# Two-layer attention and expert block on one core: row picks for two experts at once, a third place for gate and up weights, a shorter extra block

## The reference

```
def expert_dispatch(h, experts, weights, w_gate, w_up, w_down):
    ...
    def run_block(args):
        xb, e = args
        return (jax.nn.silu(xb @ w_gate[e]) * (xb @ w_up[e])) @ w_down[e]

    ys = lax.map(run_block, (xs, block_expert)).reshape(n_slots, D)
    w_sorted = weights.reshape(n_assign)[order].astype(h.dtype)
    return jnp.zeros((T, D), h.dtype).at[order // TOP_K].add(ys[dest] * w_sorted[:, None])
```

## Time and profile before

| | |
|---|---|
| median of 3 runs | 2093.99 us (2093.91 to 2096.98) |
| the profiled execution | 2094.21 us, its span 2092.4 us |
| TensorE busy | 1866.6 us (89%) |
| VectorE busy | 685.4 us (33%) |
| ScalarE busy | 515.9 us (25%) |
| chain that ended last | TensorE 72%, DMA 11%, VectorE 7% |
| moved by DMA | 550 MB, 263 GB/s over the span |

### The profile page before, as it was taken

The page is one execution under the profiler, slowest core; times in us unless marked ns, Lnnn a source line. Parts: engine busy times, 40 slices in busy tenths (PEclk is TensorE's granted clock), DMA queues, the critical chain, the costliest instruction groups (busy, mean ns, idle before and its releaser), DMA issues.

```text
span 2092.4 us, 27923 instructions
## 1 busy us (share of the span) xinstructions
PE 1866.6 (89%) x9715; PEld 999.2 (48%) x9716; DVE 685.4 (33%) x1467; ACT 515.9 (25%) x1052; POOL 153.1 (7%) x190
## 2 busy tenths in 40 slices
PE   5899999999979999977999589989978989888985
PEld 2666666668743333322333377768933333223323
DVE  2455355445442111111111475573441111111112
ACT  3344444432231101100011254442220101110111
POOL 0035021000000000000000206230000000000000
PEclk8899999999989999998999799999989999999997
DMA  6536565222256999975999333233477989999992
GB/s 219 194 141 218 203 215 206 101 75 91 81 241 281 421 421 421 421 290 237 406 421 420 138 107 96 92 106 111 146 291 311 421 363 421 420 421 421 421 421 98
DMA packets 96042, 550.47 MB, mean 263 GB/s; under 512 B 14162, under 2 KB 15650, under 8 KB 42724
## 3 DMA queue, kind: packets, MB, share of 16 engines
q1 hardware_dynamic: 83108, 526.89, 63.6%
q0 software_dynamic: 4224, 11.35, 1.9%
q10 hardware_dynamic: 8640, 11.28, 1.5%
HBM read 537.15 MB, written 12.32 MB: 263 GB/s over the span
## 4 chain that ended last, share of the span: by engine, by line
PE 72%; DMA 11%; DVE 7%; ACT 4%; issue 3%; SPq 1%; ACTq 0%; DVEq 0%; POOL 0%; POOLq 0%
PE ps L757 18%; DMA moe<-in_w_exp_gate_up_dram 9%; PE ps L479 8%; PE ps L742 8%; PE ps L769 7%; PE ps L481 7%; PE ps L480 7%; PE ps L691 2%; PE ps L647 2%; PE ps L535 2%; PE ps L749 1%; PE ps L618 1%; DVE w_lo L1225 1%; PE ps L629 1%; PE ps L763 1%
## 5 line engine op out<-in xcount | busy, mean ns | idle before, releaser
L757 PE MATMUL ps<-moe,ht 128*64 128x512 f32 x2048 | 451.4, 593 | 22.2 <-DMA moe<-in_w_exp_gate_up_dram 22.2
L757 PEld LDWEIGHTS ps<-moe,ht 128*64 128x64 f32 x2048 | 150.2, 137 | 316.1 <-issue 291.7
L479 PE MATMUL ps<-ht_hi,w_hi 128*128 128x512 f32 (+1 forms) x704 | 252.6, 359 | 1.7 <-ACT arena L1027 1.6
L1526 DVE TENSOR_TENSOR arena<-aux,ps 128x256 f32<-128x256 f32 x64 | 26.9, 421 | 687.3 <-ACT aux L1120 687.3
L481 PE MATMUL ps<-ht_hi,w_lo 128*128 128x512 f32 (+1 forms) x704 | 243.6, 346 | 0.0
L480 PE MATMUL ps<-ht_lo,w_hi 128*128 128x512 f32 (+1 forms) x704 | 243.6, 346 | 0.0
L769 PE MATMUL ps<-moe,arena 128*64 128x512 f32 x1024 | 231.4, 594 | 2.6 <-DVE arena L1547 2.6
L1225 DVE TENSOR_TENSOR w_lo<-ws,w_hi 128x1024 fp32r<-128x1024 f32 (+1 forms) x122 | 149.1, 1226 | 230.7 <-ACT w_hi L933 230.7
L742 PE MATMUL ps<-arena,ht 128*64 128x512 f32 x816 | 211.8, 629 | 4.4 <-DVE ht L1479 4.4
L933 ACT ACTIVATE w_hi<-ws 128x1024 fp32r<-128x1024 f32 (+1 forms) x122 | 125.3, 1027 | 190.2 <-PE ps L481 151.3
L479 PEld LDWEIGHTS ps<-ht_hi,w_hi 128*128 128x128 f32 x704 | 133.1, 189 | 43.7 <-issue 23.9
(11 more groups left out here) (232 smaller groups left out, 2047.8 us busy)
## 6 DMA issues: line engine op xcount, KB each, us to landing
moe<-in_w_exp_gate_up_dram SPq DMA_DIRECT2D x256, 1024.0 KB, 13.4
moe<-in_w_exp_down_dram SPq DMA_DIRECT2D x128, 1024.0 KB, 16.3
moe<-in_w_mod_dram SPq DMA_DIRECT2D x32, 1536.0 KB, 6.9
ws<-in_w_in_dram SPq DMA_DIRECT2D x92, 512.0 KB, 4.1
y_rows<-arena ACTq DMA_DIRECT2D x164, 64.0 KB, 5.6
ws<-in_w_branch_dram SPq DMA_DIRECT2D x16, 512.0 KB, 3.6
ws<-in_w_out_dram SPq DMA_DIRECT2D x16, 512.0 KB, 3.4
aux<-in_rpb_a_dram POOLq DMA_DIRECT2D x64, 64.0 KB, 3.2
```

What stands on the lines that cost most here:

```text
L479: pe.matmul(ps[:, bank, 0:cols], w[:, k, :], a_hi, start=(i == 0), stop=False)
L757: mm = pe.matmul(ps[BLK * j:BLK * j + BLK, bank, :].rearrange("p (g n) -> p g n", g=2), x[:, at:at + BLK], w[:, k, 512 * j:512 * j + 512]. ...
```

## The change

1. `pick` holds two experts (128 columns), is f32r (the one-pass format), and is multiplied with `hr_hi` and `hr_lo`, the token rows split into a rounded part and its remainder. ScalarE makes `hr_hi` in the place of `hr`; VectorE makes `hr_lo` with 2 nt new subtractions, ahead of the rest of its routing chain. `turn_x` and the copies handle the pair: picks in the pair's first expert, turns in its second.
2. `xg`, `xs`, `hid`, `hid_t` and the result buffer are single, and gate/up and down use one PSUM bank each. The freed part of `ht` and the weight buffer `ws` of the mixer form a third place for gate and up, used by expert 2 alone. The first four experts of each layer are unrolled for that (the first six in the list of loads).
3. The first extra block stands outside its loop, and the loop runs only if a second is needed. It picks with f32r too, 32 columns by 512.
4. `yg` has four places, and no fetch waits for another.

```
-AHEAD = 3
+AHEAD = 4
+PAIRS = NE // 2
+AHEAD_PAIRS = 2
...
+        wgu = [[part(moe, 32 * i + 8 * j, 8, 2, D) for j in range(4)] for i in range(2)]
+        wgu.append([part(ws_flat, 8 * j, 8, 2, D) for j in range(3)] + [part(ht_flat, 0, 8, 2, D)])
+        wd = [[part(moe, 64 + 16 * i + 8 * j, 8, 2, D) for j in range(2)] for i in range(2)]
...
+                load_gate_up(lambda w: w[l, 2], 2, range(3))
+                sp.wait_ge(g["hturn_done"].sem, g["hturn_done"].at(l, 2 * (width(l) // P) - 1))
+                load_gate_up(lambda w: w[l, 2], 2, (3,))
...
+                next_gate_up(3, 1, 0)
+                next_down(2, 0)
+                next_gate_up(4, 0, 1)
+                next_down(3, 1)
+                next_down(4, 0)
+                next_gate_up(5, 1, 3)
+                next_down(5, 1)
+                with sp.Fori(3, PAIRS) as two:
+                    for s in range(2):
+                        next_gate_up(2 * two + s, s, 2 * two + s - 2)
+                        next_down(2 * two + s, s)
...
+                def pick_x(half):
+
+                    for tile in range(nt):
+                        for rows in (hr_hi, hr_lo):
+                            mm = pe.matmul(ps[:, 7 * half, :], pick[:, tile, :], rows[:, tile, 512 * half:512 * half + 512],
+                                           start=(tile == 0 and rows is hr_hi), stop=(tile == nt - 1 and rows is hr_lo))
...
+                        more_block(BLK // MORE)
+                        with pe.If(n > BLK + MORE):
+                            with pe.Fori(BLK // MORE + 1, w_all // MORE) as b:
+                                with pe.If(n > b * MORE):
+                                    more_block(b)
+                                pe.nop(nofuse=True)
+                        pe.nop(nofuse=True)
+                    pe.nop()
+                    if s == 0:
+                        pe.wait_ge(g["pick_set"].sem, pick0 + two + 2)
+                    else:
+                        pe.wait_ge(g["xs_copied"].sem, pair0 + two + 2)
+                    next_pair = turn_x if s else pick_x
+                    next_pair(0)
+                    pe.wait_ge(g["hid_done"].sem, done + 1)
+                    turn_h(hid)
+                    next_pair(1)
+                    pe.wait_ge(g["hidt_copied"].sem, done + 1)
+                    pe.wait_ge(g["y_copied"].sem, done + 1)
+                    down(4, hid_t, wd[s], g["down_done"].sem)
...
+                for n in range(2 * nt):
+                    dve.wait_ge(g["hr_hi_set"].sem, g["hr_hi_set"].at(l, n))
+                    cols = slice(512 * (n % 2), 512 * (n % 2) + 512)
+                    v.tensor_tensor(hr_lo[:, n // 2, cols], ps[:, n % 6, :], hr_hi[:, n // 2, cols].bitcast(F32), ALU.subtract) \
+                        .then_inc(g["hr_lo_set"].sem, g["hr_lo_set"].tick(l, n))
...
                 for tile in range(nt):
-                    if tile >= 2:
-                        pool.wait_ge(g["comb"].sem, g["comb"].at(l, tile - 2))
```

More of the change, by code:

```diff
@@ L269, in hybrid_block, with gu_slot, gu_loads @@
         bias_in = [g[f"bias{i}"] for i in range(4)]
[L270 to L274, removed]
+        gu_in, wd_in = [g[f"gu_in{i}"] for i in range(3)], [g[f"wd_in{i}"] for i in range(2)]
+        yg_got = [g[f"yg_got{i}"] for i in range(4)]
+        def gu_slot(e):
+            return e if e < 3 else 1 - e % 2
+        def gu_loads(slot, before=NE):
+            return sum(gu_slot(e) == slot for e in range(before))
         def width(l):
@@ L713, in _ @@
                 mm.then_inc(g["logits_done"].sem, g["logits_done"].tick(l))
[L714 to L721, removed]
+                for n in range(2 * nt):
+                    bank = n % 6
+                    claim(bank)
+                    for c in range(4):
+                        mm = pe.transpose(ps[:, bank, c * P:(c + 1) * P], ht[:, 4 * (n % 2) + c, n // 2 * P:(n // 2 + 1) * P], ident[:, :])
+                    mm.then_inc(g["hturn_done"].sem, g["hturn_done"].tick(l, n))
+                    free[bank] = (g["hr_lo_set"], (l, n))
                 msk = r[:, 1024:1024 + 64].bitcast(BF16).rearrange("p (t e) -> p t e", e=NE)
@@ L734, in _ @@
                 pe.wait_ge(g["routed"].sem, g["routed"].at(l))
[L736 to L741, removed]
-                            mm = pe.matmul(ps[BLK * j:BLK * j + BLK, 0, :], picks[:, tile, :], hr[:, tile, 512 * j:512 * j + 512],
-                                           start=(tile == 0), stop=(tile == nt - 1))
-                    if tile == nt - 1:
+                pe.wait_ge(g["hr_lo_set"].sem, g["hr_lo_set"].at(l, 2 * nt - 1))
@@ L843, in _ @@
+                for e in range(2 * AHEAD_PAIRS):
+                    expert(e, e // 2, e % 2, gu_slot(e), gu_loads(gu_slot(e), e + 1))
+                with pe.Fori(AHEAD_PAIRS, PAIRS) as two:
+                    for s in range(2):
+                        expert(2 * two + s, two, s, 1 - s, two + s)
                 after = (l + 1, "n1") if l + 1 < DEPTH else (l, "fin")
-                pe.wait_ge(y_copied[1].sem, 16 * (l + 1) + 1)
+                pe.wait_ge(g["y_copied"].sem, NE * (l + 1) + 1)
@@ L1147, in _ @@
-                        with act.If(n > HALF):
-                            save_rows(ysb[s], act.snap(row + HALF, min_val=0, max_val=2 * NTOK), g["yt_saved"], first=HALF, rows=HALF)
-                            act.reg_add(n_tails, n_tails, 1)
-                        act.nop()
-                act.wait_ge(y_saved[0].sem, 32 * 16 * (l + 1) + 32)
-                act.wait_ge(y_saved[1].sem, 32 * 16 * (l + 1) + 32)
+                    act.nop()
+                    act.wait_ge(g["down_done"].sem, done + 1)
@@ new lines, in expert @@
+                    nc.scalar.activation(ysb, ps[:, 4, :], ACT.Copy).then_inc(g["y_copied"].sem, 1)
+                    act.wait_ge(g["y_copied"].sem, done + 2)
+                    act.wait_ge(g["yo_saved"].sem, act.snap(n_more, min_val=0, max_val=64) * 64 + 64)
+                    save_rows(ysb, row, g["y_saved"], rows=HALF)
+                    with act.If(n > HALF):
+                        save_rows(ysb, act.snap(row + HALF, min_val=0, max_val=2 * NTOK), g["yt_saved"], first=HALF, rows=HALF)
+                        act.reg_add(n_tails, n_tails, 1)
@@ L1153, in _ @@
+                    act.nop()
+                with act.Fori(0, PAIRS) as two:
+                    for s in range(2):
+                        expert(2 * two + s)
+                act.wait_ge(g["y_saved"].sem, 32 * NE * (l + 1) + 32)
                 act.wait_ge(g["yt_saved"].sem, act.snap(n_tails, min_val=0, max_val=64) * 32 + 32)
@@ L1552, in add_tile @@
+                with dve.Fori(0, PAIRS) as two:
+                    for s in range(2):
+                        expert(2 * two + s, two, s)
                 def add_tile(tile):
```

333 lines of the change are left out of this document (160 added, 173 removed).

## The result

| | before | changed |
|---|---|---|
| median | 2094.36 us (2093.91 to 2096.98, 4 runs) | 2081.49 us (2080.59 to 2084.38, 4 runs) |
| ratio | | 0.9933 (95% interval 0.9919 to 0.9948) |
| the profiled execution, its span | 2094.21, 2092.4 us | 2084.38, 2082.6 us |
| layer 0, first expert load to the end of expert 31's `down` | 569.0 us | 556.5 us |
| layer 1, the same | 528.8 us | 531.0 us |

The change makes the kernel 12.9 us faster where 33 was forecast. Layer 0 gained 12.5 us of 26.4, layer 1 lost 2.2 where 6.0 of gain was counted. The profiled execution is 2.9 us above its median.

What follows compares the result with a forecast made beforehand. TensorE set layer 0's pace and the weight loads, at 421 GB/s, late layer 1's, so idle load-queue time counted. Gains of 26.4 (layer 0), 6.0 (layer 1) and 0.8 (fetches) made 33 off 2094.2: 2061 us, range 2046 to 2085.

Steps and rivals of the forecast that it cites:

- the skip over the extra block: TensorE's jump past both copies of the extra block in experts not needing it; the sum gave it no cost.
- rival A: Jumping over the extra block's two copies costs a code fetch: 30 us slower than before, 2124 us; chance 10%.
- The price: Code fetch for each layer's first six experts: 5.6 us, like a small store under full loads; decisive from 3.1 per expert.
- The clock: TensorE's clock in new waits of up to 4.4 us per pair: should it fall, the sum stays; no separate chance.
- f32r picks 0.227 us apart: Spacing of the 16 pick products serving two experts: 3.63 us per pair in layer 0, 1.82 in layer 1.
- TensorE's pace: TensorE's time per expert pair: 27.1 us in layer 0, 26.2 in layer 1, against the loads' 31.3 and 30.5.
- Extra block: Layer 0's block after gate and up: 16.7 us instead of 21.2, 18.0 in a pair's first expert; layer 1 14.9 and 16.2.
- Start: Subtractions before each layer's first pick delay expert 0's gate and up by 6.5 us in layer 0, 4.8 in layer 1.
- Third place: Extra gate/up buffer moves 4 MB, 10 us of transfer, into idle time at each layer's start; without it, 26 us gain.
- Gathers: Tile fetches: the third tile's wait of 0.83 us goes, 0.8 us less.
- shorter extra blocks and the pick make most of it: Claim on where the gain comes from: without the third gate/up buffer the same count still gives 26 us less.

Runs made afterwards that it cites:

- the dead copies: The kernel before plus a never-run second copy of the extra block in TensorE's code of both loop experts, kept in the program: 2115.65 us, ratio 1.0093.
- the rolled kernel: The changed kernel with all 16 pairs per layer in the loop and two places for gate and up, extra block still twice: 2066.52 us, ratio 0.9854.
- the fourth of the experiments: The changed kernel with two places for gate and up instead of three, first four experts still unrolled: 2083.74 us, ratio 0.9946.

## Why the prediction was wrong, point by point

*The step that failed is the skip over the extra block.* The sum put it at nothing, and the fetch that it needs stood only in rival A, at 10%. It measured 24.3 us of gaps in ten places, and 20 us of the time come back with one copy in place of two. I had cited against it the 46 packets and the first passes without a gap. Both were true, and of another jump: one over a single copy. By the timeline's counts a copy of the extra block is 121 products in the changed kernel's layer 0 and as many weight loads (16 + 8 + 64 + 1 + 32), so 242 instructions, and in before 262. The changed kernel jumps over two copies, some 480. One copy was free in before and nearly free in the experiments (at most two gaps of 1.4 to 2.5 us in a kernel); two cost a gap at the first time behind every expert that skipped both, but for the first of a layer.

The Trainium skill (Runtime: NRT & Kernel Launch, Instruction fetch mechanics) gives blocks of 256 instructions, a window of two, and a forced fetch for a jump that leaves it. The traces agree in two points: the dead copies, 984 instructions in all (two of 262 and two of 230), bring 4 packets more, and most jumps over some 480 instructions had a gap of up to 3.0 us, those over 262 none and those over 242 few. They differ on the window: the four copies in the rolled kernel's loop are 968 instructions, and it ran all later passes with no gap and 50 packets for the whole program, so more than two blocks stayed. The section also says that kernels prefer full unrolling where possible. No run here shows a gain from unrolling alone, and with two copies it cost 17.2 us (2083.74 against 2066.52).

*The price* was set at 5.6 us by the nearest row, with the turn at 3.1 per expert. It was 1.6 to 2.9 us behind gate and up, for five experts of layer 0 and four of layer 1 in place of six each. The same count with 2 us in each of six experts gives a gain of 13.0, and with 3 us one of 1.3, both estimates; the gain was 12.9. So the mechanism of A came true and its sign did not: I had taken a fetch as either absent or as dear as a landing store, with no case at half that price.

*The clock* "is no rival of its own" held where I had looked: in the load-bound part of layer 1 gate and up take 8.49 us after a wait of 2.64, and the pair still 30.55. It failed behind the gaps, where the low-clock `down` (4.50) and picks (0.43 apart) stand among the experts that TensorE sets the pace of. By how much it adds to the loss was not measured apart from the gaps.

*The rest of the sum stands in the main.* With one copy the stages take 539.5 and 521.9 us, the forecast being 542.6 and 522.9; the time is 2061.15 against 2061.0. That it agrees to 0.2 us is luck: the stages are 4.1 us shorter than forecast, and in the profiled execution the first loads went out 4.7 us later than before (599.55 against 594.85), a start that scatters from 593.3 to 600.0 between the runs. Term by term:
- f32r picks 0.227 us apart: 0.23.
- TensorE's pace, seen without loads: a pair of layer 0 takes 27.0 us (640.01 to 667.04), 27.1 forecast; of layer 1 25.2 (1706.60 to 1731.77), 26.2 forecast.
- Extra block: 15.2 us in expert 17 against 16.7 (the terms given make 16.6), and 16.9 in expert 20 against 18.0.
- Start: gate and up of expert 0 come 3.6 us later in layer 0 and 2.9 in layer 1 after the first load, not 6.5 and 4.8. In layer 0 the pick does start 5.2 us later, as counted, but from there to gate and up it takes 9.5 us (630.96 to 640.47), where I had about 12. My own terms, 6.2 and 4.3, make 10.5, so 1.5 us of the miss is a slip in the sum; part of the rest is that only the first eight products ran at the low clock (5.7 us for the pick, not 6.2).
- Third place: 4.5 to 6.6 us against 7, where there are no gaps.
- Gathers: 0.8 forecast. Between the stages 357.9 us stand against 361.3, but the experiments scatter from 357.7 to 362.5, so nothing can be said.

*One sentence of it was wrong all the same*: "shorter extra blocks and the pick make most of it". The blocks' end alone made 29 of it, the picks nothing that shows. My count of the blocks alone was 9 us low: the empty turns held TensorE for 22.9 us, not 20.2, and the low clock within and behind the blocks of layer 0 went with them.

What stays open: why the gap behind expert 1 in the kernel with the dead copy came in two parts (2.39 and 4.25); why expert 0 of layer 1 has none with the queue full; and why some gaps stand several picks behind the jump (1.44 us in the changed kernel, 2.54 in the fourth of the experiments, 1.4 to 2.1 with one copy). No run moved the code without changing its length, so how much hangs on where a jump lands, and not on how far it goes, is not shown.

## What to carry to other kernels

Code that is skipped is not free: measure the jump in instructions, and look for gaps counted as issue behind it the first time it is taken; here they came with the DMA queues full and went with the loads made small. Give a rare block one copy, with a loop whose end is a register, before peeling it into every unrolled body; here a loop that ends with the expert's own count, put into the kernel before, brings 29 us, where the whole change brought 12.9. And where a resource sets the pace, work saved on the other engine buys only slack: it showed as no time here, though it made single stalls cheap.

## What the runs showed of the hardware that I had not expected

- Instructions that never run cost 19 us (2115.65 against 2096.5), by making the jump behind gate and up longer.
- The same code stalls 2.6 to 2.9 us per first jump of layer 0 behind experts 1 to 5 at 380 GB/s, and never over 1 us at 67 GB/s.
- Code once fetched stays: the loop of the rolled kernel, two experts with four copies of the block, 968 instructions of TensorE, had no gap after its first pass, at 50 packets.
- Taking away 22.9 us of TensorE's idle time, the empty turns of four loops, brought 29 us: work behind the idle time had run at a granted clock of 0.76.
